# Layer norms shifted early by a partial mean, with sums of squares taken inside the last units, in a hybrid decoder layer on one core

## What is computed

```python
x = LN(a*x + gate0 * 0.5 * SwiGLU_1(mod0(x)))      # d_ff 2816
x = LN(a*x + gate1 * W_out[attention | conv](mod1(x)))
x = LN(a*x + gate2 * 0.5 * SwiGLU_2(mod2(x)))
# mod_i(x) = x*(1+scale_i(c)) + shift_i(c),  a = 2**0.25
# LN: mu = mean(x); var = mean((x-mu)**2); (x-mu)*rsqrt(var+1e-5)*g + b
```

## Time and profile before

| what | value |
|---|---|
| median of 3 runs (lowest, highest) | 952.88 us (950.6, 952.88) |
| profiled execution, its own time | 953.04 us |
| span of it, first to last instruction | 951.2 us |
| PE busy | 865.2 us, 91% |
| DVE, ACT, POOL busy | 51%, 36%, 28% |
| mean granted TensorE clock | 0.957 |

### The profile page before, as it was taken

The page is one execution under the profiler, slowest core; times in us unless marked ns, Lnnn a source line. Parts: engine busy times, 40 slices in busy tenths (PEclk is TensorE's granted clock), DMA queues, the critical chain, the costliest instruction groups (busy, mean ns, idle before and its releaser), DMA issues.

```text
span 951.2 us, 16893 instructions
## 1 busy us (share of the span) xinstructions
PE 865.2 (91%) x6704; PEld 759.1 (80%) x6704; DVE 481.5 (51%) x764; ACT 342.7 (36%) x466; POOL 266.0 (28%) x319
## 2 busy tenths in 40 slices
PE   6699999997899988999987889867989999999997
PEld 3499989996799968988664556437879999999995
DVE  1543433431333387753686776564774434444436
ACT  2323332331222254455442324253463333342223
POOL 2020000000010014999999999300320000000000
PEclk9599999999899998999999989888999999999999
DMA  9958777777577434334897999994415454644401
GB/s 301 347 184 262 232 221 258 246 233 259 190 236 231 144 110 133 128 94 162 264 359 264 350 359 370 348 348 137 133 46 177 140 166 137 183 143 145 133 1 56
DMA packets 181521, 195.78 MB, mean 206 GB/s; under 512 B 11811, under 2 KB 163609, under 8 KB 181445
## 3 DMA queue, kind: packets, MB, share of 16 engines
q1 hardware_dynamic: 174541, 188.38, 61.3%
q10 hardware_dynamic: 6624, 6.33, 2.1%
q0 software_dynamic: 288, 0.14, 0.1%
HBM read 192.01 MB, written 3.17 MB: 205 GB/s over the span
## 4 chain that ended last, share of the span: by engine, by line
PE 76%; DVE 13%; DMA 4%; ACT 3%; issue 2%; SPq 1%; ACTq 0%; DVEq 0%
PE bank L1389 19%; PE bank L1390 18%; PE bank L1391 18%; PE bank L1605 5%; PE bank L1365 3%; PE bank L1630 3%; DVE wlo L956 2%; DVE kT L1194 2%; PE bank L1402 1%; PE bank L1700 1%; PE bank L1403 1%; PE bank L1404 1%; PE bank L1354 1%; DMA xrow<-in_x_sample 1%; DMA raw<-in_ffn_wg 1%
## 5 line engine op out<-in xcount | busy, mean ns | idle before, releaser
L956 DVE TENSOR_TENSOR wlo<-raw,whi 128x2048 fp32r<-128x2048 f32 (+1 forms) x80 | 190.8, 2386 | 264.1 <-ACT whi L649 264.1
L1389 PE MATMUL bank<-mh,whi 128*128 128x320 f32 x824 | 262.1, 318 | 4.5 <-DVE wlo L956 4.5
L1390 PE MATMUL bank<-ml,whi 128*128 128x320 f32 x824 | 256.5, 311 | 0.0
L1391 PE MATMUL bank<-mh,wlo 128*128 128x320 f32 x824 | 256.4, 311 | 0.0
L649 ACT CAST whi<-raw 128x2048 fp32r<-128x2048 f32 (+1 forms) x80 | 148.6, 1863 | 258.3 <-PE bank L1391 171.3
L1389 PEld LDWEIGHTS bank<-mh,whi 128*128 128x128 f32 x824 | 156.8, 190 | 15.3 <-issue 10.3
L1390 PEld LDWEIGHTS bank<-ml,whi 128*128 128x128 f32 x824 | 156.9, 190 | 0.0
L1391 PEld LDWEIGHTS bank<-mh,wlo 128*128 128x128 f32 x824 | 156.6, 190 | 0.0
L1389 PE MATMUL bank<-hh,whi 128*128 128x320 f32 x352 | 109.7, 312 | 0.0
L1390 PE MATMUL bank<-hl,whi 128*128 128x320 f32 x352 | 108.6, 309 | 0.0
L1391 PE MATMUL bank<-hh,wlo 128*128 128x320 f32 x352 | 108.6, 308 | 0.0
(11 more groups left out here) (233 smaller groups left out, 1161.2 us busy)
## 6 DMA issues: line engine op xcount, KB each, us to landing
araw<-in_w_ada SPq DMA_DIRECT2D x28, 1024.0 KB, 5.1
raw<-in_ffn_wg SPq DMA_DIRECT2D x22, 1024.0 KB, 7.5
raw<-in_ffn_wu SPq DMA_DIRECT2D x22, 1024.0 KB, 6.9
raw<-in_cache_v SPq DMA_DIRECT2D x68, 256.0 KB, 6.1
raw<-in_ffn_wd SPq DMA_DIRECT2D x16, 1024.0 KB, 6.5
raw<-in_cache_k SPq DMA_DIRECT2D x64, 256.0 KB, 4.2
raw<-in_w_in SPq DMA_DIRECT2D x10, 1024.0 KB, 5.4
raw<-in_w_ada SPq DMA_DIRECT2D x8, 1024.0 KB, 12.3
```

Source lines behind the costliest of these rows:

```text
L956: dve.tensor_tensor(wl(slot_w(phase, u))[:, 0:size], landed(phase, u)[:, 0:size], wh(slot_w(phase, u))[:, 0:size].bitcast(F32), ALU.subtra ...
L1389: pe.matmul(bank[:, b, 0:T], wh(slot)[:, c], h_, start=(start and n == 0), stop=False)
L1390: pe.matmul(bank[:, b, 0:T], wh(slot)[:, c], l_, start=False, stop=False)
L1391: ins = pe.matmul(bank[:, b, 0:T], wl(slot)[:, c], h_, start=False, stop=(stop and n == len(parts) - 1))
```

## The change

Four things. (a) POOL sums y0 to y3 only; after the first half of unit 6 of DN1 and DN2, and of unit 2 of WOUT, PE multiplies this sum, and DVE shifts y0 to y3 and the residual chunks 4 to 7 by the mean of the four. ACT squares chunks during the later units and POOL adds the squares. The norm then needs the rest of the mean, d, and takes mean(z*z) - d*d; DVE subtracts d from chunks 0 to 3 and POOL from 4 to 7. (b) The scaling by a is folded into the parameters with which ACT writes xT, and POOL's two later passes go. (c) WIN's units take other slots (unit 0 takes slot 2). DVE makes the low halves earlier: WIN's unit 1 between the adds y6 and y7 instead of inside the norm, UP2's units 0 and 1 ahead of the adds of WOUT's units 2 and 3. (d) UP2 begins with all four banks chunk by chunk; ACT loads the table for the root ahead of time; in the last norm ACT and DVE share the writing of xT.

```diff
 def slot_w(phase, u):
     if phase[0] == WIN[0]:
-        return u % 3
+        return 0 if u == WIN[2] - 1 else (2, 0, 1)[u % 3]
     if phase[0] == WOUT[0]:
...
 def slot_before(phase, u):
     if phase[0] == WIN[0]:
-        return phase[0] + u - (2 if u < 2 else 3)
+        if u == 0:
+            return -1
+        return phase[0] + u - (2 if u == WIN[2] - 1 else 3)
     if phase[0] == WOUT[0]:
-        return (WIN[0] + 9, WIN[0] + 7, WIN[0] + 8, WOUT[0])[u]
+        return (WIN[0] + 9, WIN[0] + 8, WIN[0] + 6, WOUT[0])[u]
     if phase[0] == UP2[0] and u < 4:
...
+NORM_BANKS = ((6, 4, 5), (4, 5, 6), (6, 4, 5))
...
         else:
-            sp.wait_ge(w_used, WIN[0] + (9, 9, 10, 8)[kvi - RING])
+            sp.wait_ge(w_used, WIN[0] + (7, 7, 10, 9)[kvi - RING])
         load_pages(sp, cache, kvi, numbers[8 * (k % 4 // 2) + k % 2:], range(3 if cache == "v" and j < 3 else 4))
...
-        for q in range(1, NCH - 1):
+        for q in range(1, 4):
             pool.wait_ge(y_ready, 8 * n + q + 1)
             if q > 1:
-                pool.wait_ge(ysum_step, 6 * n + q - 1)
+                pool.wait_ge(ysum_step, 5 * n + q - 1)
             pool.tensor_tensor(tmp[:, 3, :], yT[:, 0, :] if q == 1 else tmp[:, 3, :], yT[:, q, :], ALU.add).then_inc(ysum_step, 1)
-    def scale_x(n):
-        pool.wait_ge(*((h_ready[0], 2) if n == 0 else (x_ready, 8 * n)))
+    def late_sum(n, q):
+        pool.wait_ge(y_ready, 8 * n + q + 1)
+        if q == 5:
+            pool.wait_ge(shift_ready, n + 1)
+        else:
+            pool.wait_ge(ysum_step, 5 * n + 4)
+        pool.tensor_tensor(tmp[:, 3, :], yT[:, 4, :] if q == 5 else tmp[:, 3, :], yT[:, q, :], ALU.add).then_inc(ysum_step, 1)
+    def square_sum(n, q):
+        pool.wait_ge(sq_ready, 8 * n + q + 1)
+        if q > 1:
+            pool.wait_ge(sqsum_step, 6 * n + q - 1)
+        pool.tensor_tensor(tmp[:, 2, :], tmp[:, 0, :] if q == 1 else tmp[:, 2, :], tmp[:, q % 2, :], ALU.add).then_inc(sqsum_step, 1)
+    def norm(n):
+        y_sums(n)
+        for q in range(1, 5):
+            square_sum(n, q)
+        late_sum(n, 5)
+        square_sum(n, 5)
+        late_sum(n, 6)
+        square_sum(n, 6)
+        pool.wait_ge(rest_ready, n + 1)
+        pool.wait_ge(sq_ready, 8 * n + 8)
+        for q in range(4, NCH):
+            pool.tensor_tensor(yT[:, q, :], yT[:, q, :], tmp[:, 3, :], ALU.subtract).then_inc(pd_ready, 1)
+    def scale_x():
+        pool.wait_ge(h_ready[0], 2)
         pool.tensor_scalar(xT[:, :, :], xT[:, :, :], ALPHA, None, ALU.mult).then_inc(ax_ready, 1)
...
+    pool.tensor_scalar(par1[:, 96:112], par1[:, 96:112], ALPHA, None, ALU.mult).then_inc(fold_ready, 1)
+    norm(0)
     pool.wait_ge(w_used, DN1[0] + DN1[2])
...
     pool.memset(qo[:, :, :, :], 0.0).then_inc(q_zero, 1)
-    scale_x(1)
     pool.wait_ge(st_in, 2)
...
         pool.wait_ge(conv_ready, c)
-    y_sums(1)
-    scale_x(2)
-    y_sums(2)
+    norm(1)
+    norm(2)
...
             act.wait_ge(w_used, n + more)
-        if phase is WIN and u == 2:
+        if phase is WIN and u == 0:
             act.wait_ge(ada_used, ADAN)
...
         up_pairs(act, body)
-    def down(phase, nxt):
+    def square(n, q):
+        if q < 4:
+            act.wait_ge(yc_ready, 2 * n + q // 2 + 1)
+        else:
+            act.wait_ge(y_ready, 8 * n + q + 1)
+        if q >= 2:
+            act.wait_ge(sqsum_step, 6 * n + max(q - 2, 1))
+        act.activation(tmp[:, q % 2, :], yT[:, q, :], ACT.Square).then_inc(sq_ready, 1)
+    def down(phase, nxt, n):
         for u in range(phase[2]):
...
                 hi(nxt, u + SLOTS - phase[2])
-    def norm(n):
-        for q in range(4):
-            act.wait_ge(yc_ready, 4 * n + q + 1)
-            act.activation(squares(q), yT[:, 2 * q:2 * q + 2, :], ACT.Square).then_inc(sq_ready, 1)
-        act.wait_ge(var_ready, n + 1)
-        act.activation(tmp[:, 0, :], bank[:, 1, 0:T], ACT.Sqrt, bias=con[:, C_EPS:C_EPS + 1]).then_inc(std_ready, 1)
+            if u == 7:
+                for q in range(4):
+                    square(n, q)
+            if u == 9:
+                square(n, 4)
+                square(n, 5)
+    def norm(n, first, meanwhile=lambda: None):
+        act.wait_ge(ld_con, 16)
+        act.activation(warm[:, :], con[:, C_EPS:C_EPS + 1], ACT.Sqrt)
+        for q in range(first, NCH):
+            square(n, q)
+        act.wait_ge(mean_ready, n + 1)
+        act.wait_ge(sqsum_step, 6 * n + 6)
+        act.copy(tmp[:, 3, :], bank[:, NORM_BANKS[n][1], 0:T]).then_inc(rest_ready, 1)
+        act.wait_ge(rest_ready, n + 1)
+        act.activation(tmp[:, 0, :], tmp[:, 3, :], ACT.Square).then_inc(dsq_ready, 1)
+        act.wait_ge(vd_ready, n + 1)
+        act.activation(tmp[:, 0, :], tmp[:, 0, :], ACT.Sqrt, bias=con[:, C_EPS:C_EPS + 1]).then_inc(std_ready, 1)
+        meanwhile()
         for q in range(NCH):
...
                 act.copy(mh[:, q, :], uT[:, q, :]).then_inc(mh_ready, 1)
+            elif q % 2:
+                continue
             act.wait_ge(xn_ready, 8 * n + q + 1)
...
     up(0, UP1, DN1)
-    down(DN1, WIN)
-    hi(WIN, 2)
-    norm(0)
+    down(DN1, WIN, 0)
+    norm(0, 6, lambda: hi(WIN, 2))
...
                 prompt_exp(head_scored(slot - 1))
-            if cc and u + 3 < WIN[2]:
+            if cc and u + 3 < WIN[2] - 1:
                 hi(WIN, u + 3)
+            if cc and u + 2 == WIN[2] - 1:
+                hi(WIN, u + 2)
             if slot == STATE_AT:
...
     hi(UP2, 0)
+    for q in range(4):
+        square(1, q)
     hi(UP2, 1)
-    norm(1)
+    norm(1, 4)
     up(1, UP2, DN2)
-    down(DN2, None)
-    norm(2)
+    down(DN2, None, 2)
+    norm(2, 6)
 @block.vector
...
+    def shift(n):
+        sums = bank[:, NORM_BANKS[n][0]:NORM_BANKS[n][0] + 1, 0:T].to_broadcast([P, 2, T])
+        dve.wait_ge(shift_ready, n + 1)
+        for q in (2, 3):
+            x = xT[:, 2 * q:2 * q + 2, :]
+            dve.scalar_tensor_tensor(x, sums, -2.0, x, ALU.mult, ALU.add).then_inc(xs_ready, 1)
+        for q in (0, 1):
+            y = yT[:, 2 * q:2 * q + 2, :]
+            dve.scalar_tensor_tensor(y, sums, -2.0, y, ALU.mult, ALU.add).then_inc(yc_ready, 1)
+        dve.wait_ge(xs_ready, 2 * n + 2)
     def down(sub, phase, nxt, n0):
-        dve.wait_ge(ax_ready, sub + 1)
+        dve.wait_ge(*((ax_ready, 1) if sub == 0 else (x_ready, 16)))
         for u in range(phase[2]):
...
                 ada_turn(down_ada(u), down_ada(u), b=2)
+            if u == 6:
+                shift(sub)
             if third == 2:
...
                                  (n_ready, n0 + nb + 1) if cc == 0 else (w_used, phase[0] + u + 1))
-    def norm(n, meanwhile=lambda: None):
-        dve.wait_ge(mean_ready, n + 1)
-        dve.wait_ge(y_ready, 8 * (n + 1))
-        for q in range(4):
+                    if nxt is not None and last and cc == 0:
+                        lo(nxt, u + SLOTS - phase[2])
+    def norm(n):
+        d = tmp[:, 3:4, :].to_broadcast([P, 2, T])
+        def centre(q):
             y = yT[:, 2 * q:2 * q + 2, :]
-            dve.tensor_tensor(y, y, bank[:, 0:1, 0:T].to_broadcast([P, 2, T]), ALU.subtract).then_inc(yc_ready, 1)
-        for q in range(4):
-            dve.wait_ge(sq_ready, 4 * n + q + 1)
-            two = squares(q)
-            dve.tensor_tensor(two[:, 0, :], two[:, 0, :], two[:, 1, :], ALU.add).then_inc(sqsum_ready, 1)
-        meanwhile()
+            dve.tensor_tensor(y, y, d, ALU.subtract).then_inc(yd_ready, 1)
+        dve.wait_ge(rest_ready, n + 1)
+        centre(0)
+        dve.wait_ge(var_ready, n + 1)
+        dve.wait_ge(dsq_ready, n + 1)
+        dve.tensor_tensor(tmp[:, 0, :], bank[:, NORM_BANKS[n][2], 0:T], tmp[:, 0, :], ALU.subtract).then_inc(vd_ready, 1)
+        centre(1)
         dve.wait_ge(std_ready, n + 1)
         link(dve.reciprocal(tmp[:, 1, :], tmp[:, 0, :]))
-        dve.wait_ge(fold_ready, 1)
+        dve.wait_ge(fold_ready, 2)
         def scale(q):
             y = yT[:, q, :]
+            dve.wait_ge(*((yd_ready, 2 * n + q // 2 + 1) if q < 4 else (pd_ready, 4 * n + q - 3)))
             dve.tensor_tensor(y, y, tmp[:, 1, :], ALU.mult).then_inc(xn_ready, 1)
...
                     low(q - 1, 8 * (n + 1 + (n == 1)) + q, uT)
+            elif q % 2:
+                dve.wait_ge(xn_ready, 8 * n + q + 1)
+                dve.tensor_scalar(xT[:, q, :], yT[:, q, :], par1[:, 72 + 8 * n + q:73 + 8 * n + q],
+                                  par1[:, 96 + 8 * n + q:97 + 8 * n + q], ALU.mult, ALU.add).then_inc(xd_ready, 1)
         if n < 2:
...
     down(0, DN1, WIN, 0)
-    norm(0, lambda: lo(WIN, SLOTS - 1))
+    norm(0)
     dve.wait_ge(ada_out, ADAN)
...
             slot = 2 * u + cc
-            if cc == 0 and 1 <= u < WIN[2] - 2:
+            if cc == 0 and 1 <= u < WIN[2] - 3:
                 lo(WIN, u + 2)
+            if cc == 0 and u == WIN[2] - 2:
+                lo(WIN, u + 1)
             if win_kind(u) == 1:
...
     low(NHP - 1, 24)
-    dve.wait_ge(ax_ready, 2)
```

(58 more changed lines are left out.)

## The result

The changed kernel took 963.19 us, the median of 4 runs (961.42 to 965.58), beside 951.74 (4 runs, 949.91 to 952.88) of the kernel before on the same chip: a ratio of 1.0123, with an interval of 1.0098 to 1.0147. Measured again beside other runs of the kernel before it was 961.12 against 950.87, 1.0107 [1.0087, 1.0127] (after_again). It is slower, by 11.5 and 10.3 us or 1.1 to 1.2%, both intervals wholly above 1; 959.2 was forecast, 6.2 more than before. The profiled execution took 964.09 us against 953.04.

The account below looks back on a forecast made before the run. PE was taken to bound the kernel in the windows read, leaving gains at the norms. Stage terms gave +0.3 and clock falls +5.9 on the profiled 953.04: 959.2 us, range 949 to 966, the forecast's own 955.5 to 965.

Parts of the forecast that it names:

- The three waits: PE waits for POOL's add of y3: 2.6 us in DN1's unit 6, 4.9 in WOUT's unit 2, 3.7 in DN2's unit 6.
- The rival in which POOL goes first: Where a DVE split stands beside a POOL add, POOL goes first in all three places, pauses shorten: 948.8 us; chance 0.12.
- the early sum: Rival: y3's sum is ready in time, so 12.9 us of waits and the clock falls vanish: near 943 us; chance 0.03.
- The clock in the pauses: PE's clock falls behind new pauses of 2.6, 4.9, 3.8 and 3.7 us: 1.7 for each long one, 0.8 short, +5.9.
- The rival in which the clock holds: Pauses among dense products trigger no clock fall, as at 351.92: 953.3 us, no change; chance 0.21.
- The short pause in DN1: PE's 2.6 us wait for y3's sum in DN1's unit 6, with 0.8 us taken for the clock behind it.
- The first norm and WIN's start: First norm's reciprocal 6.6 us after PE's last product: -2.3; WIN's start without POOL's scaling holding DVE's split: -5.9.
- POOL's memsets lie beside the norm's later half: First norm: POOL's memsets were put at nothing in the sum.
- PE doesn't pause, so the clock stays: WIN's start: no wait at unit 2, so the clock holds; -2.7 us taken, beside -3.2 for the split.
- The start of UP2: Four banks together need 14.1 us of PE; unit 2 starts at 18.0 instead of 17.3, +0.7, with 3.8 us idle.
- Second norm and tail: Second norm's 14.0 us becomes 11.2, -2.8; tail's reciprocal 3.3 earlier but xT writing +1.0, net -2.3.
- The table load: Rival: squares evict the root's table, so each norm loads twice more, 1.28 us each: near 965 us; chance 0.07.

Follow-up runs that it names:

- after_again: The changed kernel unedited, measured again beside other runs of the kernel before, with a second profile: 961.12 us against 950.87, 1.0107.
- e5_scale_only: Kernel before with only the residual's scaling folded into ACT's write parameters and POOL's two later passes gone: 947.13 us against 950.34, 0.995.
- e6_all: Changed kernel with shift half a unit later, POOL's memsets behind DVE's first ml, UP2 begun with three banks then one: 945.93 us against 950.87, 0.9943.
- e6_again: The changed kernel with late shift, later memsets and three banks then one, measured once more: 945.73 us against 950.22, 0.9938.
- e2_memset_later: Changed kernel, but POOL's three memsets wait until the first norm's modulation is done: 956.97 us, 1.0072 of the kernel before.
- e7_all_order: Changed kernel with late shift, later memsets, three banks, and in WOUT DVE's shift before its split of UP2's unit 0: 946.29 us, 0.9946 of kernel before.
- e8_act_order: Changed kernel with late shift, later memsets, three banks; in WOUT ACT's UP2 unit 1 cast and root table load precede the squares: 946.31 us, 0.9965.
- the two other edits: In the changed kernel beside the late shift: POOL's memsets after the first norm's modulation, and UP2 begun with three banks then one; all together 0.9943 and 0.9938.

## Why the prediction was right, and where it was off

**The three waits.** Right, to 0.12 us each, and with them most of the loss. The step that carried it was to take the end of POOL's add of y3 from the old trace, ask whether the program orders ahead of it change, and compare it with half a unit of products. The matmul of the shift was put at 0.56 and took 0.78, and 1.41 at the lower clock. That DVE's split goes first in WOUT and holds the add was right too: it took 2.84 us. The rival in which POOL goes first did not occur. Nor was the early sum ready.

**The clock in the pauses.** The step was right and the sizes near: 2.5 us in WOUT and 1.6 in DN2 by the run with the waits filled, 1.5 in UP2 by the run with three banks, where 1.7 was taken for each. One such fall isn't the same in each execution: behind UP2's pause of 3.76 us the way to DN2 took 142.44 to 143.55 us in five profiles, 1.5 to 2.6 above the 140.91 without a fall. The rival in which the clock holds fell. The short pause in DN1 was put at 0.8, between none and a fall; it cost nothing in four profiles and something in one. The Trainium skill, page "TensorE: Matmul & The Clock Gate", Part 1, puts the ramp below 1% of a typical kernel's span and advises against fitting a number of slow matmuls. It says this of the ramp at a kernel's start, and the prediction stretched it to pauses inside a kernel. Here the falls behind the three long pauses come to 5.6 us, 0.6% of the span, which is half of the loss. In the forecast they decided the sign, with +0.3 for all the rest; in the run they didn't, since without them the change would still lose 5 us or more of its 11.0.

**The first norm and WIN's start.** Forecast -8.2, measured -5.3: this is the largest error of the sum. The step that failed is the sentence that puts "POOL's memsets lie beside the norm's later half" at nothing. They did lie beside it, and held DVE's tensor_scalar: +1.8 us in the chain, as the run with later memsets shows. The clock then fell, +1.5, where the prediction let it stay. It did so in all five profiles with 4.1 us of idleness there, but also in three of seven with 2.3 (e5_scale_only, e6_all, e6_again; not in before, e2_memset_later, e7_all_order and e8_act_order). So "PE doesn't pause, so the clock stays", which looked at WIN's unit 2 alone, was not safe without the memsets either. With them away the norm gains 2.8 (forecast 2.3), and WIN's start 5.9 (5.9) where the clock holds and 4.4 where it falls. I had named the cover and not asked whether it excludes the covered. The Trainium skill, page "SBUF — State Buffer", section "Who interferes with whom", has the rule that was missed: a tensor_scalar can run in a mode that takes both pairs of ports, and then shares none with GpSimd, while a DVE operation with two inputs in SBUF excludes only what reads there. The trace agrees with both halves, though it doesn't show in which mode the tensor_scalar ran: beside the memset it took 2.24 us instead of 0.41, and the pair of two-input products ahead of it, the second of which began after the memset did, took 1.02 us, as it does with the memsets away. So the prediction's "POOL and a two-input DVE operation exclude each other" is too wide: it had seen this for POOL's adds and scaling, which read SBUF, and not for a memset.

**The start of UP2.** Forecast unit 2 at 18.0 us with 3.8 idle, measured 19.63 with 3.76. The idleness was right; the 14.1 us for four banks were not, since the clock is low behind the second norm in both kernels (0.50 from 699.1 to 702.5 after) and I took the products at full pace. At full clock, in the run with the waits filled, the four banks took 18.07 - 3.76 = 14.3. This is 1.6 us.

**Second norm and tail.** -3.1 and -2.5, forecast -2.8 and -2.3. Right.

**The table load.** No second load was seen. ACT's timeline of the second norm:

```profile
682.54 1.28 ACT L781 ACT_TABLE_LOAD   x1
683.84 0.20 ACT L781 ACTIVATE warm<-con 128x1 f32<-128x1 f32 x1
683.95 0.46 ACT L761 ACTIVATE tmp<-yT 128x320 f32<-128x320 f32 x1
```

The squares run on behind the root's table, and the trace has 11 loads, as many as that of before. That rival's time, 965, is near what was measured, with nothing of its mechanism in the trace: a right time is no sign of a right cause.

Together: -0.6 in DN1, +2.9 in the first norm and WIN, +1.2 in WOUT, +1.4 in UP2, +0.8 in the attention, -0.9 in the rest, +4.8 on a forecast of +6.2. So the three waits and the falls behind them were foreseen, and four smaller terms were set too favourably. That the second profile's +7.8 lies nearer to the forecast is luck: its attention took 3.5 us less.

**What stays open.** Why the clock fell behind the 2.48 us in DN1 in one profile and not in four, and behind the 2.3 us of the first norm in three of seven; what would take the 5.7 us out of WOUT and the norm behind it, which no run got back; and why the attention stage is 172 us in some executions and 175 in others.

## What to carry to other kernels

Work that is moved ahead of its old place is free only if its last input is there: take the time of that input from the old trace before you set the place, and put the consumer behind it by the shortest stretch that covers the difference; here half a unit of products brought the change from 1.1 to 1.2% slower to 0.3% slower, and with the two other edits it was 0.6% faster than the kernel before. Where more work stands behind the new place than the units left can cover, as in WOUT, the later place only moves the wait. An operation on one engine that "lies beside" a chain on another must be checked for whether the two can run at once, a plain memset too. And a pause of the matrix engine is paid twice once it is long enough, with the length and with the slow products behind it, so here pauses of 3.7 and 4.9 us cost 5.3 and 7.4 within their stages.

## What the runs showed of the hardware

- A memset on POOL, which reads nothing, held DVE's tensor_scalar: 2.24 us instead of 0.41, and 0.40 with the memsets away.
- At the four places of the changed kernel where PE sat idle for 3.69 to 4.90 us the granted clock was at 0.50 each time, in every profile, with full pace 3 to 6 us after work began again. Behind 2.29 to 2.48 us it fell in some executions and not in others: in one of five in DN1, three of seven behind the first norm, four of four behind the second. Behind 2.00 us at the second norm it fell in the kernel before, and behind 2.01 in e5_scale_only it did not. Behind the second norm with the pause in WOUT filled and 1.50 us it did not.
- DVE's split of a weight unit and POOL's adds hold each other at whichever place they meet. Taken from beside the add of y3 (2.83 us became 0.88), the split met an add of squares (0.87 became 2.72); taken earlier by 2 us, another split met three of them (4.83 us instead of 2.6) and took 2.97 itself instead of 2.29.
